# A chunked RWKV7 scan with its second head's 64-wide systems on the other half of the partitions, paired products, and square roots taken on 12 columns instead of 768

## The chip, the cores and the metric

The kernel runs on one core of one Trainium2 chip. The metric is the device time of one execution in microseconds (us); smaller is better. All numbers below are of the kernel before the change.

## The reference, cut to what matters

The whole program is a two-layer diffusion block in float32 (512 latent positions, 256 context positions, width 1024). Layer 0 mixes by windowed attention and a Hyena filter, layer 1 by RWKV7, and both have a SwiGLU. The change touches the RWKV7 recurrence and the normalisation behind it, and nothing else:

```
kk = rw_heads(k * k_k)
kk = kk / jnp.maximum(jnp.sqrt(jnp.sum(jnp.square(kk), axis=-1, keepdims=True)), 1e-12)
k_dir = k[None] * (1.0 + (a - 1.0) * k_a)
...
sa = jnp.einsum('ebhvk,ebhk->ebhv', s, kk_t)
s = s * w_t[..., None, :] - sa[..., :, None] * (kk_t * a_t)[..., None, :] + v_t[..., :, None] * k_t[..., None, :]
y = jnp.einsum('ebhvk,ebhk->ebhv', s, r_t)
...
var = jnp.mean(jnp.square(y - mean), axis=-1, keepdims=True)
yn = (y - mean) * lax.rsqrt(var + RW_GN_EPS)
```

There are 16 heads of 64 channels and two directions e (forward and backward), each over 768 positions (context, then latent).

## The kernel before, in words

A tile is a pair of heads h = 0, 1, one on partitions 0 to 63 and one on 64 to 127, so there are 8 tiles. The 768 positions are cut into 12 chunks of TC = 64, which lie in pairs: pair j = 0 to 5, and p = 0, 1 says which chunk of the pair. Inside a chunk the recurrence is a triangular system of 64 by 64, solved by doubling: blocks of 16 are inverted on POOL, then two levels (16 to 32, 32 to 64) are products on PE. What is left is a chain over the chunks.

Five engines each run a list of instructions in an order that is written out by hand and joined by semaphores (`PEM`, `DV`, `AC`, `PO` are the lists of marks). `ROUNDS` runs over (i, n, c) = (it, it+1, it+2): in one round tile i is solved and finished ("back"), tile n is prepared ("front"), and for tile c the keys are normalised. So rounds overlap three tiles. PSUM has eight banks: the back products take turns on bank pairs 0-1 and 2-3 (`BACK`), the front ones on 4-5 and 6-7 (`FRONT`). A product may start when the one two places before it in its list has been read out.

PE's list in a round, with the lines of the profile:

- `lora` L2143: `l00 l01` (and, after `w16`, `l10 l11`), 4 matmuls of 64 rows by 128 columns of the array, 384 moving columns, for direction e on the rows `H2[e]`. ACT applies tanh, POOL halves it, DVE forms the running sum `scan_e` (L2472), ACT the exponentials `ep_e en_e`.
- `squares` L2159, 24 matmuls of 64x64 each: `w16 x16 y16 w32 y32` for both directions (10 of them), then `ok obv` for both (the solved keys and values); at the round's end `BV_0 BV_1`. Head h goes to bank b+h, and chunk p has rows p and columns p of the array.
- `A_0`, `A_1` (L2169, `gram`): the system matrices of tile n; DVE masks them (`mA_e`, L2513), SP carries the blocks of 16 through DRAM to POOL and their inverses back to `XY`, which `w16` of the next round waits for.
- `m_0 m_1` (L2251), `n_0 n_1` (L2264, L2268), `r` (L2278), `yt` (L2288): transition matrices, chunk states, readout of the state, outputs from inside the chunk.
- `chain` L2198: `c0_k c1_k` for k = 1 to 10, each followed on DVE by `st0_k st1_k` (L2529). Between them stand `cg` (three matmuls of 512 columns), `K_e` (L2169), `CD_e` (L2181), and the transposes `tV tB_e tK_e` (L2150), which ACT reads out (L2384).
- `ys` (L2346), `kT_0`, `kk` (L2355), `kT_1`, `mean` (L2362), `BV_0 BV_1`, `var` (L2368).

DVE's end of a round: `ysum`, `cen`, then for tile c `kmax` (L2609), `krec` (L2611, the reciprocal of 128x768) and `kmul`, then for tile i `rec` (L2616, the reciprocal of 128x512), `f1 f2 z`. Then comes the next round's mask of `w16` (L2463). `HONES` is a 128x128 matrix of ones in two blocks of 64: its product with squares gives every channel of a head the head's sum, so the root and the reciprocal are taken on 64 equal copies.

Of the kernel before, what the change touches and what calls it, by code (L numbers as in the profile page):

```python
# [8 lines left out]
ALU = mybir.AluOpType  # L9
# [4 lines left out]
L = 512  # L14
C = 256
T = L + C
# [13 lines left out]
CH = 64  # L30
# [58 lines left out]
def hybrid_dit_kernel(nc, a, out):  # L89
# [3 lines left out]
    with ctx:  # L93
# [1744 lines left out]
        def mixes_dve(v):  # L1838
# [65 lines left out]
        OKT = WI  # L1904
# [30 lines left out]
        class Marks(dict):  # L1935
# [23 lines left out]
        DV = Marks(dve_done, (  # L1959
# [113 lines left out]
        def scan_pool(pool):  # L2073
            sub = Chain(pool, sub_step)
            for _, n, _ in ROUNDS:
# [6 lines left out]
                if n:  # L2082
                    pool.wait_ge(pe_done, PEM["obv_1", n - 1])
# [26 lines left out]
        def scan_pe(pe):  # L2110
# [739 lines left out]
```

## Time and profile before

| what | us |
|---|---|
| median of 3 runs | 2684.48 (2682.06 to 2690.17) |
| the profiled execution's own time | 2696.97 |
| its span | 2695.2 |
| the stage that the change touches, first `kk` to last `z` | 1581.4 to 2208.2 |
| one round in its middle (from `lora` to `lora`) | 71.91 |

Names in the profile are those of the memory arenas: `scan_front`, `scan_tokens`, `scan_back`, `scan_small`, and PS for PSUM. A float32 matmul of the program appears as two records of PE (a transpose as one), each with a weight load of its own; the time of a record is from its start to its modelled end, and records overlap. What a stream of them takes is read from the starts. "issue" as the end of a wait means that nothing in the trace held the engine.

### The profile page before, as it was taken

To read this page: it belongs to the slowest core of one execution; us is meant where nothing else is said; L and a number is where in the kernel's file an instruction comes from. 1 tells how busy PE (TensorE), PEld (TensorE's weight loads), DVE (VectorE), ACT (ScalarE), POOL (GpSimd) and SP (SyncE) were. 2 spreads that over 40 slices of the span, in tenths; PEclk is the share of its full clock that TensorE was granted. 3 is DMA by queue.
4 is the path that set the end of the run, shared out by engine and by line. 5 is a ranking of instruction groups with operands and counts; after the bars stand their busy time and mean duration, and the time that the engine had idled before them with its cause. 6 is when DMAs were issued, how large, how long until landed. Compare 5 with 4: busy or idle time off the path is not lost. (4 is left out here: it accounts for less than half of the span.)

```text
span 2695.2 us, 53413 instructions
## 1 busy us (share of the span) xinstructions
PE 2350.2 (87%) x23840; PEld 1946.5 (72%) x23840; DVE 1019.5 (38%) x1482; ACT 640.1 (24%) x952; POOL 836.0 (31%) x699
## 2 busy tenths in 40 slices
PE   5899977989699999999489957888888858999997
PEld 3778754555499999999269936776777746788786
DVE  4100076890400000122692045777777641200123
ACT  4110165421400000122321123333333212211111
POOL 2233200100144444343054412222222205466562
PEclk8999988989799999999599968999999978999998
DMA  5555510001021111111123411111211111222231
GB/s 219 209 203 203 209 49 17 0 31 48 16 71 62 62 62 62 56 62 48 26 79 110 138 51 39 37 40 39 40 40 38 22 64 63 77 94 93 86 98 67
DMA packets 139278, 204.26 MB, mean 76 GB/s; under 512 B 87783, under 2 KB 97511, under 8 KB 131912
## 3 DMA queue, kind: packets, MB, share of 16 engines
q1 hardware_dynamic: 139080, 201.26, 23.1%
q8 instruction: 168, 2.75, 0.4%
q14 instruction: 30, 0.25, 0.0%
HBM read 183.93 MB, written 17.30 MB: 75 GB/s over the span
## 5 line engine op out<-in xcount | busy, mean ns | idle before, releaser
L258 POOL CAST TMP_r<-WR 128x1024 fp32r<-128x1024 f32 x120 | 126.9, 1058 | 757.3 <-DMA WR<-in_ffn_w_dram 437.9
L277 PE MATMUL PS<-H_r,TMP_r 128*128 128x384 f32 (+1 forms) x1088 | 331.1, 360 | 15.1 <-DVE Y_r L492 15.1
L277 PE MATMUL PS<-Y_r,TMP_r 128*128 128x384 f32 (+1 forms) x1088 | 330.3, 358 | 3.7 <-DVE H_r L492 3.7
L260 POOL TENSOR_TENSOR WR_r<-WR,TMP_r 128x1024 fp32r<-128x1024 f32 x120 | 290.0, 2416 | 9.6
L415 DVE TENSOR_TENSOR P<-TMP,PS 128x768 f32 (+1 forms) x44 | 36.1, 821 | 563.0 <-PE PS L277 563.0
L277 PEld LDWEIGHTS PS<-H_r,TMP_r 128*128 128x128 f32 x1088 | 202.1, 190 | 33.6 <-DVE Y_r L492 17.3
L277 PEld LDWEIGHTS PS<-Y_r,TMP_r 128*128 128x128 f32 x1088 | 201.8, 190 | 19.3 <-DVE H_r L492 4.0
L277 PE MATMUL PS<-H_r,WR_r 128*128 128x384 f32 x736 | 191.6, 342 | 0.0
L268 POOL CAST TMP_r<-WR 128x1024 fp32r<-128x1024 f32 x68 | 86.4, 1271 | 322.8 <-DMA WR<-in_rw_w_rkv_dram 165.3
L270 POOL TENSOR_TENSOR WR_r<-WR,TMP_r 128x1024 fp32r<-128x1024 f32 x68 | 165.3, 2431 | 5.4
L398 ACT ACTIVATE TMP<-PS 128x768 f32<-128x768 f32 (+1 forms) x44 | 31.1, 706 | 526.5 <-PE PS L277 526.5
L588 PE MATMUL PS<-H_r,TMP_r 128*128 128x384 f32 x704 | 153.0, 340 | 3.2 <-DVE H_r L626 2.2
L2159 PE MATMUL PS<-scan_back 64*64 64x64 f32 x3840 | 122.6, 223 | 28.0 <-DVE scan_back L2463 17.5
L2159 PEld LDWEIGHTS PS<-scan_back 64*64 64x64 f32 x3840 | 119.6, 139 | 34.2 <-DVE scan_back L2463 21.8
L277 PE MATMUL PS<-Y_r,WR_r 128*128 128x512 f32 x352 | 139.4, 396 | 0.0
L277 PEld LDWEIGHTS PS<-H_r,WR_r 128*128 128x128 f32 x736 | 133.5, 189 | 0.0
L588 PEld LDWEIGHTS PS<-H_r,TMP_r 128*128 128x128 f32 x704 | 126.4, 189 | 3.8 <-DVE P L415 2.5
L1731 PE MATMUL PS<-P_r,TMP_r 128*128 128x384 f32 (+1 forms) x448 | 113.1, 344 | 1.0 <-DVE X_r L1856 1.0
L588 PE MATMUL PS<-Y_r,TMP_r 128*128 128x512 f32 x352 | 109.7, 393 | 2.4 <-DVE Y_r L626 2.4
L1622 PE MATMUL PS<-H_r,TMP_r 128*128 128x384 f32 x352 | 94.8, 352 | 8.7 <-POOL WR_r L260 8.5
L1622 PE MATMUL PS<-H_r,WR_r 128*128 128x384 f32 x352 | 92.5, 345 | 0.0
L626 DVE TENSOR_TENSOR H_r<-P,H_r 128x768 fp32r<-128x768 f32 x44 | 43.3, 1022 | 129.1 <-ACT H_r L619 129.1
(289 smaller groups left out, 4433.1 us busy)
## 6 DMA issues: line engine op xcount, KB each, us to landing
WR<-in_ffn_w_dram SPq DMA_DIRECT2D x88, 512.0 KB, 3.5
TMP<-in_mod_w_dram SPq DMA_DIRECT2D x40, 1024.0 KB, 4.9
WR<-in_down_dram SPq DMA_DIRECT2D x44, 512.0 KB, 3.6
WR<-in_mix_w_in_dram SPq DMA_DIRECT2D x24, 512.0 KB, 7.0
WR<-in_rw_w_rkv_dram SPq DMA_DIRECT2D x24, 512.0 KB, 4.2
P<-in_mod_w_dram SPq DMA_DIRECT2D x4, 2048.0 KB, 21.9
vkr_dram<-extra SPq DMA_DIRECT2D x16, 384.0 KB, 4.8
scan_front<-vkr_dram SPq DMA_DIRECT2D x16, 384.0 KB, 3.3
```

Source lines behind the costliest of these rows:

```text
L258: nc.gpsimd.tensor_copy(hi, raw).then_inc(weights_hi, 1)
L260: nc.gpsimd.tensor_tensor(lo, raw, hi.bitcast(F32), ALU.subtract).then_inc(weights_split, 1)
L268: nc.gpsimd.tensor_copy(hi, raw).then_inc(weights_hi, 1)
L270: nc.gpsimd.tensor_tensor(lo, raw, hi.bitcast(F32), ALU.subtract).then_inc(weights_split, 1)
L277: last = nc.tensor.matmul(PS[:, bank + b, 0:h1 - h0], w, x[:, h0:h1], start=k + p == 0, stop=k == CT - 1 and p == 2)
L398: nc.scalar.activation(as_halves(GATE[:, u, 0:d.n], d.n), halves(bank, d.n), ACT.Silu)\
L415: nc.vector.tensor_tensor(as_halves(dst, d.n), as_halves(GATE[:, u, 0:d.n], d.n), halves(4 * u + 2, d.n), ALU.mult).then_inc(d.unit_free, 1)
L588: last = nc.tensor.matmul(PS[:, bank, 0:h1 - h0], w[:, at:at + 128], x[:, q % 4, h0:h1], start=k + p == 0, stop=k == FT - 1 and p == 2)
L626: nc.vector.tensor_tensor(d.lo[:, q % 4, :], P[:, q % FT, 0:d.n], d.hi[:, q % 4, :].bitcast(F32), ALU.subtract).then_inc(hid_split, 1)
L1622: last = nc.tensor.matmul(PS[:, 2 * u + b, 0:HALF], w, x[:, HALF * b:HALF * b + HALF], start=k + p == 0, stop=k == CT - 1 and p == 2)
L1731: last = nc.tensor.matmul(PS[:, 2 * (t % SLOTS) + b, 0:h1 - h0], wt, x[:, k, h0:h1], start=k + p == 0, stop=k == CT - 1 and p == 2)
L2159: last = nc.tensor.matmul(PS[pr, b + h, 64 * j:64 * j + 64], lhs(pr, h, j), rhs(pr, h, j), start=True, stop=True)
```

## The change

Eight edits of the scan stage; the rest of the program is the same.

1. `lora(n, k)` makes both directions at once, with the two row halves of the array in turn.
2. For head 1 the systems of chunk p lie on the partitions of chunk 1-p (`H2[p ^ h]`), in `A_e`, `BV_e`, the solved `OO`, and the transposed keys `KINT`. For that `turned` replaces the transposes `kT_e`: 6 transposes of 64 partitions and 12 matmuls with the identity.
3. `solve` makes keys and values in one product of 128 moving columns (`oo_0 oo_1 oo_2` for `ok_e obv_e`), 48 matmuls instead of 96. `transition` does so for `m` and `r` (`mr_0 mr_1 mr_2`), `gram_keys` for the keys and readout (`KD_e`); `gram_rest` is `CK_e`.
4. `yt` and `ys` add up in PSUM: `YTS` and `ysum` go, ACT copies `ys`.
5. Sums of squares go the other way round (`turned_sums`): 128x12 and 128x8 values instead of 128x768 and 128x512. Root and reciprocal are taken of these, ACT widens them to 64 columns each (`kwide`, `vwide`), PE transposes them back (`kr`, `vr`), DVE multiplies from PSUM.
6. `ends_e first_e rate_e acc_0` move from DVE to ACT.
7. Orders: `scan_0` ahead of the `w16` masks on DVE, `scan_1` right behind them; `rt kd kt` of tile n later; `n_1` last before the chain, `cg` before `n_0`.
8. Masks of 1024 and 768 elements become four of 512, 512, 512 and 256 (`mK mD mC mL`), one set behind `st_2`, `st_3`, `st_5`, `st_6`.

```diff
         PEM = Marks(pe_done, (
...
-            (0, "c0_8 c1_8"), (1, "tK_0"), (0, "c0_9 c1_9"), (1, "tB_1"), (0, "c0_10 c1_10"), (1, "tK_1"),
-            (0, "ys"), (1, "kT_0"), (2, "kk"), (1, "kT_1"), (0, "mean"), (1, "BV_0 BV_1"), (0, "var")))
+            (1, "l00 l10"), (0, "w16_0 w16_1"), (1, "l01 l11"), (0, "x16_0 y16_0 x16_1 y16_1 w32_0 w32_1 y32_0"),
+            (1, "A_0"), (0, "y32_1 oo_0 oo_1"), (1, "A_1"), (0, "oo_2 mr_0 mr_1 cg mr_2 n_0 yt n_1"),
+            (0, "c0_1 c1_1"), (1, "KD_0"), (0, "c0_2 c1_2"), (1, "CK_0"), (0, "c0_3 c1_3"), (1, "KD_1"),
+            (0, "c0_4 c1_4"), (1, "CK_1"), (0, "c0_5 c1_5"), (1, "tV"), (0, "c0_6 c1_6"), (1, "tB_0"),
...
+            (0, "c0_10 c1_10"), (1, "kT_0"), (0, "ys"), (1, "kT_1"), (0, "mean"), (2, "kk"), (1, "BV_0"), (0, "var"),
+            (2, "kr"), (1, "BV_1"), (0, "vr")))
...
+            (0, "st0_3 st1_3"), (1, "mC_0 mL_0"), (0, "st0_4 st1_4"), (1, "accr"), (0, "st0_5 st1_5"), (1, "mK_1 mD_1"),
+            (0, "st0_6 st1_6"), (1, "mC_1 mL_1"), (0, "st0_7 st1_7 st0_8 st1_8 st0_9 st1_9 st0_10 st1_10 cen"),
...
                 for h in range(2):
-                    last = nc.tensor.matmul(PS[:, b + h, 0:HALF], w[r, :], x[r, HALF * h:HALF * h + HALF],
-                                            start=True, stop=True)
-                PEM.done(last, name, n)
+                    for e, r in enumerate(H2):
+                        last = nc.tensor.matmul(PS[:, b[e] + h, 0:HALF], w[r, :], x[r, HALF * h:HALF * h + HALF],
+                                                start=True, stop=True)
...
+            def turned(n, e):
+                name = f"kT_{e}"
                 b = front(name, n)
                 for j in range(6):
+                    c = slice(64 * j, 64 * j + 64)
+                    nc.tensor.transpose(PS[:, b, c], KIN[e][H2[0], 128 * j:128 * j + 128], ident[H2[0], H2[0]])
+                    for p in range(2):
+                        t = 128 * j + 64 * p
+                        last = nc.tensor.matmul(PS[H2[1 - p], b + 1, c], KIN[e][H2[1], t:t + 64], ident[H2[1], H2[1]],
+                                                start=True, stop=True)
...
+            def solve(i, name, turns):
+                b = back(name, i)
+                for k, (e, j) in enumerate(turns):
+                    for h in range(2):
+                        for q, qr in enumerate(H2):
+                            last = nc.tensor.matmul(PS[H2[q ^ h], b + h, 128 * k:128 * k + 128], XY[qr, 2 + e, h, j, :],
+                                                    beside(KINT[qr, e, h, j, :], BVT[qr, e, h, j, :]),
+                                                    start=True, stop=True)
...
+            def turned_sums(bank, src, groups):
+                for j in range(groups):
+                    last = nc.tensor.matmul(PS[:, bank, 2 * j:2 * j + 2], src[:, 128 * j:128 * j + 128],
+                                            HONES[:, 0:128:64], start=True, stop=True)
...
+                    pe.wait_ge(dve_done, DV["n_1", i])
+                    chain(i, 1)
...
+                    AC.done(nc.scalar.activation(KROOT, PS[:, front_bank("kk", c), 0:12], ACT.Sqrt), "kroot", c)
...
+                    act.wait_ge(dve_done, DV["krec", c])
+                    AC.done(nc.scalar.activation(KS.rearrange("p (k t) -> p k t", t=TC),
+                                                 KROOT.unsqueeze(2).broadcast_to([128, 12, TC]), ACT.Copy), "kwide", c)
...
-                    DV.done(nc.vector.reciprocal(KS, KS), "krec", c)
...
+                    DV.done(nc.vector.reciprocal(KROOT, KROOT), "krec", c)
```

At the end of a round PE's list was this (the last `c` pair, the transposes L2150, `ys` L2346, `kk` L2355, `mean` L2362, `BV` L2159, `var` L2368, and the next round's `lora` L2143):

```order
L2198 MATMUL PS<-scan_back 64x64 x4
L2150 MATMUL PS<-ident,scan_front 128x128 x6
L2346 MATMUL PS<-scan_small,scan_back 64x64 x32
L2150 MATMUL PS<-ident,scan_front 128x128 x6
L2355 MATMUL PS<-scan_front 128x384 x2
L2150 MATMUL PS<-ident,scan_front 128x128 x6
L2362 MATMUL PS<-scan_small,scan_front 128x512
L2159 MATMUL PS<-scan_tokens 64x64 x48
L2368 MATMUL PS<-scan_small,scan_front 128x512
L2143 MATMUL PS<-TMP,scan_small 128x384 x4
```

In the changed program the same place reads so (`c` L2311, `turned` L2171 and L2174, `ys` L2294, `mean` L2422, `kk` and `var` L2301, `BV_e` L2224, `kr` L2436, `vr` L2444, `lora` L2145):

```order
L2311 MATMUL PS<-scan_back 64x64 x4
L2171 MATMUL PS<-ident,scan_tokens 128x64
L2174 MATMUL PS<-ident,scan_tokens 64x64 x2
...
L2294 MATMUL PS<-scan_small,scan_back 64x64 x32
...
L2422 MATMUL PS<-scan_small,scan_front 128x512
L2301 MATMUL PS<-scan_front 128x2 x6
L2224 MATMUL PS<-scan_tokens,scan_front 64x64 x24
L2301 MATMUL PS<-scan_front,scan_small 128x2 x4
L2436 MATMUL PS<-ident,scan_front 128x128 x6
L2224 MATMUL PS<-scan_tokens,scan_front 64x64 x24
L2444 MATMUL PS<-ident,scan_small 128x128 x4
L2145 MATMUL PS<-TMP,scan_small 128x384 x4
```

The pair L2171, L2174 stands six times on each side of `ys` in place of six transposes of 128x128, `kk` has moved behind `mean`, and `kr` and `vr` are new.

DVE's list from `cen` into the next round was:

```order
L2606 SCALAR_TENSOR_TENSOR scan_small<-PS,scan_small 128x512
L2609 TENSOR_SCALAR scan_front<-scan_front 128x768
L2611 RECIPROCAL scan_front<-scan_front 128x768
L2613 TENSOR_TENSOR scan_front<-scan_front 128x768
L2616 RECIPROCAL scan_small<-scan_small 128x512
L2618 SCALAR_TENSOR_TENSOR scan_small<-scan_small,PC 128x512
L2620 SCALAR_TENSOR_TENSOR scan_small<-scan_small,PC 128x512
L2622 TENSOR_TENSOR Y<-scan_small 128x512
L2463 TENSOR_TENSOR scan_back<-PS,scan_small 128x768 x2
L2472 SCALAR_TENSOR_TENSOR scan_front<-extra,scan_front 128x768
```

and is now (`cen` L2755, `kmax` L2758, `krec` L2760, `rec` L2763, `kmul` L2766, `f1 f2 z` L2770 to L2775, `scan_e` L2589, the `w16` masks L2580):

```order
L2755 SCALAR_TENSOR_TENSOR scan_small<-PS,scan_small 128x512
L2758 TENSOR_SCALAR scan_small<-scan_small 128x12
L2760 RECIPROCAL scan_small<-scan_small 128x12
L2763 RECIPROCAL scan_small<-scan_small 128x8
L2766 TENSOR_TENSOR scan_front<-scan_front,PS 128x768
L2770 SCALAR_TENSOR_TENSOR scan_small<-scan_small,PC,PS 128x512
L2772 SCALAR_TENSOR_TENSOR scan_small<-scan_small,PC 128x512
L2775 TENSOR_TENSOR Y<-scan_small 128x512
L2589 SCALAR_TENSOR_TENSOR scan_front<-extra,scan_front 128x768
L2580 TENSOR_TENSOR scan_back<-PS,scan_small 128x768 x2
L2589 SCALAR_TENSOR_TENSOR scan_front<-extra,scan_front 128x768
```

The two long reciprocals have become short ones, `kmul` and `f1` read PSUM, and the running sum stands ahead of the masks.

## Rows read from the trace of the kernel before

**Rows 1.** Stretches of one round, then the last round; columns as headed.

```profile
core 0: us, PE busy (x) PEld busy (x) DVE busy (x) ACT busy (x) POOL busy (x), PEclk, DMA share, GB/s
1859.63:1885.98 26.35, 22.54 (x545) 19.50 (x545) 24.02 (x25) 7.73 (x10) 3.26 (x4) 0.94 0.03 8
1885.98:1906.45 20.47, 15.00 (x721) 14.20 (x722) 15.88 (x21) 3.92 (x5) 4.23 (x5) 1.00 0.15 24
1906.45:1921.63 15.18, 14.61 (x353) 10.94 (x345) 10.07 (x27) 4.44 (x6) 12.20 (x30) 1.00 0.32 91
1921.63:1927.47 5.84, 5.80 (x83) 4.25 (x82) 0.69 (x1) 5.37 (x7) 0.00 (x0) 1.00 0.50 72
1927.47:1931.54 4.07, 4.00 (x98) 3.18 (x99) 4.03 (x3) 2.97 (x5) 0.00 (x0) 1.00 0.49 45
2144.96:2208.16 63.20, 46.19 (x1306) 38.55 (x1306) 31.70 (x46) 5.75 (x8) 0.00 (x0) 0.80 0.01 3
```

**Rows 2.** The same view: five whole rounds, `lora` to `lora`.

```profile
1715.47:2073.74 358.27, 309.09 (x8922) 258.95 (x8921) 273.10 (x371) 122.12 (x150) 95.53 (x190) 0.98 0.19 37
```

**Rows 3.** Timeline of DVE: start, duration, then what.

```profile
1856.75 4.95 DVE L2611 RECIPROCAL scan_front<-scan_front 128x768 f32<-128x768 f32 x1
1862.62 3.35 DVE L2616 RECIPROCAL scan_small<-scan_small 128x512 f32<-128x512 f32 x1
1868.18 1.81 DVE L2463 TENSOR_TENSOR scan_back<-PS,scan_small 128x768 f32<-128x768 f32 x2
1869.91 1.75 DVE L2472 TENSOR_TENSOR_SCAN scan_front<-extra,scan_front 128x768 f32<-128x768 f32 x1
1909.87 0.69 DVE L2584 TENSOR_TENSOR scan_small<-PS,scan_front 128x512 f32<-128x512 f32 x1 [2.18 <-PE PS L2299]
```

**Rows 4.** Timeline of PE at the round's start: `lora`, then `w16`.

```profile
1859.63 2.84 PE L2143 MATMUL PS<-TMP,scan_small 64*128 64x384 f32 x8
1862.40 3.01 PE L2159 MATMUL PS<-scan_back,scan_tokens 64*64 64x64 f32 x96
```

**Rows 5.** Timeline of PE in the attention: scores on two row halves.

```profile
363.03 0.70 PE L735 MATMUL PS<-P 64*128 64x256 f32 x4
```

**Rows 6.** Timeline of PE, last round: `r`, and `yt`'s last record.

```profile
2174.61 1.11 PE L2278 MATMUL PS<-scan_tokens,scan_back 64*64 64x64 f32 x63
2176.99 0.27 PE L2278 MATMUL PS<-scan_tokens,scan_back 64*64 64x64 f32 x1 [1.27 <-issue]
...
2180.46 0.27 PE L2288 MATMUL PS<-scan_tokens 64*64 64x64 f32 x1 [1.38 <-issue]
```

**Rows 7.** Timeline of PE: a third of `cg`, the chain, `ys`.

```profile
1907.76 1.02 PE L2298 MATMUL PS<-TMP,scan_small 128*128 128x512 f32 x2
...
1918.46 0.87 PE L2150 MATMUL PS<-ident,scan_front 128*128 128x128 f32 x6
1919.26 0.45 PE L2198 MATMUL PS<-scan_back 64*64 64x64 f32 x8
1919.64 0.87 PE L2150 MATMUL PS<-ident,scan_front 128*128 128x128 f32 x6
1921.63 2.08 PE L2346 MATMUL PS<-scan_small,scan_back 64*64 64x64 f32 x64
```

**Rows 8.** Timelines of ACT (read-out, table load) and of POOL.

```profile
1924.55 0.81 ACT L2384 ACTIVATE scan_back<-PS 128x768 f32<-128x768 f32 x1 [0.31 <-PE PS L2150]
1925.38 1.28 ACT L2427 ACT_TABLE_LOAD   x1
...
1862.72 1.63 POOL L2081 TENSOR_SCALAR scan_front<-scan_front 128x768 f32<-128x768 f32 x2 [14.51 <-ACT scan_front L2374]
```

**Rows 9.** First tile: DVE's `mA_1`, then PE's first `w16`.

```profile
1610.71 0.96 DVE L2513 TENSOR_TENSOR scan_tokens<-PS,extra 128x768 f32<-128x768 f32 x1 [1.68 <-PE PS L2169]
1645.46 5.39 PE L2159 MATMUL PS<-scan_back,scan_tokens 64*64 64x64 f32 x96 [9.39 <-DMA scan_back<-inv_dram]
```

**Rows 10.** The stretch view again: chain to `var` of the last round.

```profile
2180.46:2200.00 19.54, 14.97 (x154) 9.69 (x155) 6.86 (x23) 1.82 (x3) 0.00 (x0) 0.66 0.01 2
```

More of the change, by code:

```diff
@@ L1977, in hybrid_dit_kernel @@
         FRONT_FREE = {"l00": (AC, "t00"), "l01": (AC, "t01"), "l10": (AC, "t10"), "l11": (AC, "t11"),
[L1978 to L1982 removed]
+                      "A_0": (DV, "mA_0"), "A_1": (DV, "mA_1"), "cg": (AC, "gt"), "KD_0": (DV, "mD_0"),
+                      "CK_0": (DV, "mL_0"), "KD_1": (DV, "mD_1"), "CK_1": (DV, "mL_1"), "kk": (AC, "kroot"),
+                      "kr": (DV, "kmul"), "BV_0": (AC, "bv_0"), "BV_1": (AC, "bv_1")}
+        BACK = "w16_0 w16_1 x16_0 y16_0 x16_1 y16_1 w32_0 w32_1 y32_0 y32_1 oo_0 oo_1 oo_2 mr_0 mr_1 mr_2 n_0 yt n_1".split()
+        BACK_FREE = {"oo_0": (AC, "oo_0"), "oo_1": (AC, "oo_1"), "oo_2": (AC, "oo_2"), "mr_0": (DV, "r_0"),
+                     "mr_1": (DV, "r_1"), "mr_2": (DV, "m5_1")}
         def front_bank(name, n):
@@ new lines, in transition @@
+            def transition(i, e):
+                name = f"mr_{e}"
+                b = back(name, i)
+                pe.wait_ge(act_done, AC[f"oo_{e}", i])
+                for j in range(4):
+                    for p, pr in enumerate(H2):
+                        for h, hr in enumerate(H2):
+                            last = nc.tensor.matmul(PS[hr, b + p, 128 * j:128 * j + 128], OO[pr, e, h, j, 0, :],
+                                                    beside(CD[pr, e, h, 0, j, :], TOKB[pr, e, j, hr]),
+                                                    start=True, stop=True)
+                PEM.done(last, name, i)
@@ new lines, in transition_rest @@
+            def transition_rest(i):
+                b = back("mr_2", i)
+                pe.wait_ge(act_done, AC["oo_2", i])
+                for e in range(2):
+                    for j in range(4, 6):
+                        at = 128 * e + 64 * (j - 4)
+                        for p, pr in enumerate(H2):
+                            for h, hr in enumerate(H2):
+                                last = nc.tensor.matmul(PS[hr, b + p, at:at + 64], OO[pr, e, h, j, 0, :],
+                                                        TOKB[pr, e, j, hr], start=True, stop=True)
+                PEM.done(last, "mr_2", i)
@@ new lines, in outputs_carried @@
+            def outputs_carried(i):
+                pe.wait_ge(dve_done, DV["st1_10", i])
+                for ch in range(NLAT):
+                    for e in range(2):
+                        was = order(e)[order(e).index(ch) - 1]
+                        at = 64 * (ch // 2)
+                        for hr in H2:
+                            last = nc.tensor.matmul(PS[hr, 2 + ch % 2, at:at + 64], NE[hr, e, was % 2, was // 2, :],
+                                                    RSTEP[hr, ch % 2, e, ch // 2, :], start=False,
+                                                    stop=ch >= NLAT - 2 and e == 1)
+                PEM.done(last, "ys", i)
@@ L2225, in scan_pe @@
[L2225 to L2232 removed]
+                        level("x16", e, "w16", Ym, Wm)
@@ L2245, in scan_pe @@
[L2245 to L2253 removed]
+                        pe.wait_ge(act_done, AC["kT_1", i])
@@ L2291, in scan_pe @@
-                    PEM.done(last, "yt", i)
-                    pe.wait_ge(dve_done, DV["r", i])
-                    chain(i, 1)
+                    solve(i, "oo_2", [(e, j) for e in range(2) for j in (4, 5)])
+                    transition(i, 0)
+                    transition(i, 1)
                     b = front("cg", i)
```

559 lines of the change are left out of this document (310 added, 249 removed), and 18 rows, old and new, of tables (AC, DV, PEM).

## The prediction

> **What bounds the kernel now.** I read, in this order, the table of stretches (who is busy when), the timelines of PE and DVE in one round (who waits for whom), and the two ends of the stage. The table cuts one round into five stretches [rows 1]. No engine is full: in the 71.9 us of the round PE is busy 62.0 us and DVE 54.7. The bound changes hands. In the first stretch (26.35 us, `lora` to the first solve) DVE is busy 24.0 us: the two reciprocals of the old round's end (4.95 and 3.35 us) run into it, and the masks of `w16` start at 1868.18, 8.55 us after `lora`, though PE had finished `w16` at 1865.4 [rows 3, 4]. From there on PE is the longer one: in the stretch from `c_1` to `ys` it is busy 14.6 of 15.2 us.
>
> In the second stretch (20.5 us) PE is busy only 15.0 us. The rest is mostly waits that nothing in the trace explains. The last round shows their pattern: products that fill all four 64x64 quadrants run at 13.5 ns a record (63 records in 1.11 us, less the last one's 0.27), yet the ends of two such waits lie 3.47 us apart (1.27 us up to 2176.99, 1.38 us up to 2180.46), with the 128 records of `yt` in between [rows 6]. So a long run of these costs 3.4 us for 128, or 26.7 ns a record, whatever the array could do. I read this as the supply of instructions. The Trainium skill (Runtime: NRT & Kernel Launch, Instruction fetch mechanics) says that instructions come in blocks of 256, which is 128 matmuls with their weight loads, and agrees; it also calls the cost mostly hidden, and there the trace differs, with 1.27 and 1.38 us each. By the page's word the sum below would lose two stalls of about 1.4 us in a round, some 22 us in eight.
>
> Five whole rounds take 358.27 us, 71.65 each [rows 2].
>
> **The change, stretch by stretch, in a middle round.** All times count from `lora`. I take 0.1 us for a hand-over between engines, 0.9 us for a DVE pass over 768 elements (two in 1.81 [rows 3]), 0.6 to 0.7 us over 512 (0.69), 0.8 us for an ACT read-out (0.81 [rows 8]), and 1.4 us for a diagonal `squares` (96 records in 3.01 [rows 4]).
>
> *`lora` to first solve: 26.35 before, 20.0 after.* Two row halves do work side by side: 4 records of 256 columns start 0.107 us apart ((0.70 - 0.38)/3) [rows 5], so eight of 384 columns take 1.6 us, not 2.84. Then tanh 0.8, POOL 0.8 (1.63 for two [rows 8]) and `scan_0` 1.75 end at 5.1; the masks of `w16` behind it end at 6.9, `scan_1` at 8.6. `x16 y16` go in turns with their freed banks until 13.5, `kin_0 ba_0` to 15.2, the `w32` masks to 17.0, `bt_0` to 17.9, `y32_0` to 18.8. PE meanwhile has `A_0` and `y32_1` until 20.0. The removed reciprocals (8.3 us) are thus worth 6.3 us here, since what replaces them is in the last stretch.
>
> *To `c_1`: 20.5 before, 19.8 after.* Solve: 96 records of 128 columns replace 192. At 13.5 ns for 64 columns they take 27 ns, 2.6 us in all against four times 1.4. But `A_1` waits for `bt_1` (23.9), `mr_1` for ACT's read of `oo_2` (27.0), and `cg`, now ahead of the states, takes about 3.05 (three parts of 1.0 us [rows 7]) and ends at 30.95. Then `mr_2`, `n_0`, `yt`, `n_1` are 352 records of the fast kind. Between 352 x 13.5 ns = 4.8 us and 352 x 26.7 = 9.4 I take 7.8, since `cg` gives the supply time for one block. `n_1` is now last, so its read-out (0.96 with two hand-overs) lies ahead of the chain: `c_1` at 39.8.
>
> *`c_1` to `ys`: 15.2 before, 18.9 after.* `cg` is gone from it. But the masks behind `st_5` (1.25 us) now free the bank for `tV`, and `tV` stands ahead of `c_6`; the same holds for `st_6`, `tB_0` and `c_7`. Each of these steps costs c 0.4, st 0.5, masks 1.0 to 1.25, transposes 0.8, together about 2.9 us, against 1.18 us for a step before (the transposes start at 1918.46 and 1919.64 [rows 7]). With the others `c_10` is at 15.0 and `kT_0`, which waits until ACT has done `kc ksq tB_1`, at 15.9. `turned` has no equal in the trace. It changes between 64*128 and 64*64 six times there and back. In the chain one such pair of changes costs what 1.18 us leaves above the work: 8 records of 30 ns and 6 of 0.10 to 0.12 leave 0.2 to 0.35 us. So `turned` takes 6 x 0.2 + 0.6 = 1.8 at least and 6 x 0.35 + 1.3 = 3.4 at most, or, if a change between shapes with the same 64 rows were free, 1.1. I take 3.0, near the upper end, because its items are short and each waits for the one before to leave the array.
>
> *`ys` to end of `mean`: 5.8 before, 6.1 after:* 2.05 (`ys` [rows 7]), 3.0 (`turned` again, which covers ACT's copy of `ys`), 1.05 (`mean`, 512 columns as a part of `cg`).
>
> *End of `mean` to the next `lora`: 4.1 before, 7.3 after.* This is the price of the short reciprocals. `cen` 0.7, `sq` 0.65 (two thirds of the elements of a read-out), table load 1.28 [rows 8], `kroot` 0.25, `bv_0` 0.75, `groot` 0.2, `kwide` 0.85, `kr` 0.85 with its hand-over, `BV_1` 0.8, `bv_1` 0.9. The next `lora` needs the bank that `bv_1` frees. `kk` and `var` (12 and 8 records of at most 0.12 us) lie beside ACT's part.
>
> Sum: 20.0 + 19.8 + 18.9 + 6.1 + 7.3 = 72.1 us against 71.9 for this round and 71.65 on average: about 0.45 us more in each of five rounds, 2.2 in all. The gains and losses of the middle rounds cancel.
>
> **The ends of the stage** do not. Before the first round, `mA_1` of tile 0 ends at 1611.7 and `w16` starts 33.8 us later (1645.46), on the blocks' way through DRAM and POOL, which the change leaves alone [rows 9]. After it there is no 4.95 us reciprocal in front of the first `scan`, less on DVE ahead of `mA_1` and twice the speed for `lora`: it comes about 6.7 us sooner, of which I keep 5.5, since PE has to be through the front of tile 0 too. The first round then takes 0.6 us more than before. The next to last has no keys to normalise: 1.5 us less. The last one (63.2 us [rows 1]) gains about 8.5: 2.6 since `f1 f2 z` and the masks of `w16` no longer wait for 3.35 us of `rec`, 3.3 in solve and states, 0.5 in the chain, 2.1 at `var` to `z` (3.35 + 0.7 less two short steps, the widening and the transposes).
>
> One term more: the granted clock. It was 0.98 over five rounds [rows 2] and 0.94 in the first stretch, where PE waits for DVE [rows 1]. With two levels, 2.4 and 1.2 GHz, a mean of 0.98 is 4% of the time at the lower one, 2.9 us of a round, and costs 1.4. After the change PE waits at more places, so I add a third of that, an estimate: 0.5 us a round, 3.5 in all.
>
> Total: -5.5 + 0.6 + 2.2 - 1.5 - 8.5 + 3.5 = -9.2 us. The profiled execution was 2696.97 us, 12.5 above the median of 2684.48; taken off the median, 2675.3 us.
>
> **Rivals.**
> - *`turned` is cheap.* If its changes of shape cost nothing, 1.1 us each: twice 1.9 us in seven rounds, 26.6 us less: 2649. For it: both shapes use 64 rows. Against it: the only change seen, of columns and rows, costs 0.2 to 0.35. Chance 0.15.
> - *No wait for instructions behind `cg`.* If the supply gets far enough ahead during `cg`, two waits of 1.4 us go in each round: 22 us less, 2653. Against it: in the last round such waits come every 128 records [rows 6], and 352 stand here. This is also what the page's word would give. Chance 0.08.
> - *Solve and value products don't spread over four quadrants.* The new placing has both row halves write to one bank at once, where the old four-quadrant products had a bank for each. Then records of 128 columns cost 54 ns instead of 27: 0.85 us on the path at `oo_2`, 0.7 at `BV_1`, in eight rounds 12.4 us more: 2688. Against it: `squares` writes so today, at 30 ns, two at a time. The Trainium skill has this as a rule (TensorEngine Tiling, Gotcha 1: different row tiles cannot access the same PSUM bank simultaneously); the trace shows two doing it in halves of a bank, and nothing here shows four. Chance 0.10.
> - *Slower: the chain with its waits pulls the clock down.* PE would stand still at `kr`, `A_1`, ahead of `c_1` and at the masks, 1 to 2 us each. If 4 us of its work in each round ran at the lower of its two levels, that is 4 us more in a round, 28 in seven, less the 3.5 in the sum: 2700. It decides from about 2.9 us a round on. For it: in the last chain, with nothing between its steps, the clock was 0.66 [rows 10]. Chance 0.15.
> - The forecast itself: 0.52.
>
> **Numbers.** What a measurement can tell from no change is about 0.3%, or 8 us: below 2676.4 and above 2692.5. My case's own range is 2662 to 2688 (1.5 us a round either way in seven rounds, 2 us at the ends), so it gives about half of itself to faster and nearly all the rest to the same. Faster 0.49 (0.15 and 0.08 of it the first two rivals), same 0.31, slower 0.20 (0.13 of it the clock, the rest the banks and my own case). Range 2650 to 2696.
>
> **What would show it.** Right: `RECIPROCAL` of 128x12 and 128x8 well below 0.5 us; `lora` at 1.6 us; solve at 27 ns a record; `turned` 3 us; `c_6` and `c_7` 2.9 us after the step before; 7 us from `mean` to `lora`; a round of 71 to 73 us; first `w16` 5 us sooner, last round 55 us. Wrong: a round below 69 us (then `turned` or the supply of instructions was overpriced) or over 74 (then look at PEclk, at `mr_1`, and at ACT between `cen` and `kr`).

## The result and the profile after

The change made the kernel slower: 2725.14 us (median of four runs, 2717.38 to 2729.26) against 2685.75 in the same rounds for the kernel before, a ratio of 1.0134 with a 95% interval of 1.0115 to 1.0153. The prediction said 2675.3, at most 2696. The interval lies clear of 1: the change costs 1.2 to 1.5%. The profiled execution took 2726.47 us with a span of 2724.5, and the mean granted clock was 0.912 (before 0.932).

The view of stretches over the same cuts as in [rows 1], then the last round from its `w16` on, then the five middle rounds as in [rows 2]:

```profile
core 0: us, PE busy (x) PEld busy (x) DVE busy (x) ACT busy (x) POOL busy (x), PEclk, DMA share, GB/s
1873.29:1894.81 21.52, 19.22 (x544) 16.78 (x545) 17.09 (x17) 9.80 (x15) 4.69 (x4) 0.96 0.03 10
1894.81:1915.30 20.49, 14.77 (x577) 11.49 (x573) 15.98 (x21) 4.28 (x5) 7.06 (x13) 1.00 0.15 22
1915.30:1935.56 20.26, 16.54 (x298) 13.93 (x299) 10.36 (x30) 5.50 (x7) 9.96 (x22) 0.83 0.39 91
1935.56:1942.96 7.40, 7.40 (x103) 5.89 (x103) 0.00 (x0) 2.22 (x3) 0.00 (x0) 0.77 0.19 20
1942.96:1951.60 8.64, 7.10 (x127) 6.17 (x126) 2.25 (x5) 5.09 (x9) 0.00 (x0) 0.70 0.01 2
...
2181.00:2238.00 57.00, 45.59 (x1159) 38.07 (x1157) 24.99 (x47) 5.93 (x9) 0.00 (x0) 0.77 0.01 3
...
1712.84:2108.77 395.93, 330.14 (x8162) 275.16 (x8161) 228.16 (x365) 135.21 (x191) 108.48 (x190) 0.88 0.17 34
```

The reader is to see two things. The five rounds hold fewer records than before (8162 against 8922) and less DVE work (228 against 273 us), and still take 37.7 us more: 79.2 each, not 71.65. And the clock of the last three stretches, 1.00 before, is now 0.83, 0.77 and 0.70. With the levels 1.2 and 2.4 GHz, 0.88 over 395.93 us is 24% of the time at the lower one, 19 us of a round. Before it was 2.9.

Where the 29.3 us between the two spans came about (the medians are 39.4 us apart, since the profiled execution of the kernel before took 12.5 us more than its median; where those 12.5 lie isn't known):

| part of the program | forecast | measured |
|---|---|---|
| up to the first middle round (1712.84 against 1715.47) | -4.9 | -2.6 |
| five middle rounds (395.93 against 358.27) | +4.7, clock term included | +37.7 |
| the last two rounds (2108.77 to the end of `z` at 2238.56; before 2073.74 to 2208.16) | -9 | -4.6 |
| behind the stage (485.9 against 487.0) | 0 | -1.1 |

The timeline of PE, the same round from `turned` on (a pair L2171, L2174 stands six times, the first three and the last one are shown):

```profile
1933.02 0.27 PE L2171 MATMUL PS<-ident,scan_tokens 64*128 64x64 f32 x1 [0.55 <-ACT scan_tokens L2472]
1933.22 0.33 PE L2174 MATMUL PS<-ident,scan_tokens 64*64 64x64 f32 x4
1933.49 0.27 PE L2171 MATMUL PS<-ident,scan_tokens 64*128 64x64 f32 x1
...
1935.55 0.27 PE L2174 MATMUL PS<-ident,scan_tokens 64*64 64x64 f32 x2
...
1935.67 3.21 PE L2294 MATMUL PS<-scan_small,scan_back 64*64 64x64 f32 x63
...
1947.62 1.51 PE L2436 MATMUL PS<-ident,scan_front 128*128 128x128 f32 x6 [1.54 <-ACT scan_front L2548]
1949.07 1.56 PE L2224 MATMUL PS<-scan_tokens,scan_front 64*64 64x64 f32 x48
1950.56 1.11 PE L2444 MATMUL PS<-ident,scan_small 128*128 128x128 f32 x4
```

`turned` takes 2.6 us, a pair every 0.46 us, and `ys` behind it 3.21 us where it took 2.08 [rows 7]. `kr`, `BV_1` and `vr` behind the wait run at half speed (`BV_0`, the same work, took 0.93 us at 1944.17). The waits of PE over the five rounds, with their total, number and longest:

```profile
PE PS L2153 <- DVE scan_tokens L2629: 8.9, 5, 1.9
PE PS L2162 <- DVE scan_back L2580: 8.8, 10, 0.9
PE PS L2185 <- DVE scan_front L2602: 7.6, 5, 1.5
PE PS L2153 <- DVE scan_front L2638: 6.8, 5, 1.4
PE PS L2436 <- ACT scan_front L2548: 6.6, 5, 1.5
PE PS L2283 <- issue: 5.7, 4, 1.7
PE PS L2311 <- DVE scan_back L2663: 5.3, 5, 1.1
```

None is longer than 1.9 us, and these seven are 49.7 us in all, 10 us of a round (13.1 with the smaller ones). L2153 is `tV` and `tB_0` at the masks, L2185 is `A_1` at `bt_1`, L2436 is `kr` at the widening, L2311 is `c_1` at `n_1`. Waits of this length stood in the kernel before too, 9.6 us of a round in all, and its clock was 0.98. The longest, from the same view over its five rounds:

```profile
PE PS L2268 <- issue: 9.2, 6, 2.2
```

So the waits alone don't explain the clock.

### The profile page after: what moved, and what is told of

The parts are those of the page before. It is cut to its first block and busy times, and to the rows that moved or that the text cites. A ratio compares the mean times of both kernels' runs of the same rounds, so it can differ in the third digit from the quotient of the medians.

```text
span 2724.5 us, 51046 instructions
## 1 busy us (share of the span) xinstructions
PE 2374.1 (87%) x22624; PEld 1965.6 (72%) x22624; DVE 945.4 (35%) x1475; ACT 661.4 (24%) x1016; POOL 850.0 (31%) x699
## 5 line engine op out<-in xcount | busy, mean ns | idle before, releaser
L2085 POOL TENSOR_SCALAR scan_front<-scan_front 128x768 f32<-128x768 f32 x32 | 36.1, 1147 | 249.9 <-ACT scan_front L2451 249.9
L1622 PE MATMUL PS<-Y_r,TMP_r 128*128 128x384 f32 x352 | 91.0, 339 | 0.0
L343 PE MATMUL PS<-Hraw,WR 128*128 128x384 f32 x256 | 85.6, 498 | 5.8 <-DVE Hraw L1425 5.8
```

The lines of the kernel that those rows point to most:

```text
L343: last = nc.tensor.matmul(PS[:, 2 * s + h, 0:HALF], WR[:, s, k, :], outproj.rhs(k)[:, HALF * h:HALF * h + HALF], start=k == 0, stop=k == C ...
L1622: last = nc.tensor.matmul(PS[:, 2 * u + b, 0:HALF], w, x[:, HALF * b:HALF * b + HALF], start=k + p == 0, stop=k == CT - 1 and p == 2)
L2085: PO.done(nc.gpsimd.tensor_scalar(x, x, 0.5, 0.5, ALU.mult, ALU.add), f"s{e}{k}", n)
```

## The experiments

All ratios are to the kernel before, timed beside each kernel. Its median there lay between 2683.66 and 2691.03 us, so a difference of two medians from different groups of runs can be off by up to 7 us. Where it matters, the difference of the ratios is given beside it. "Five rounds" is the stretch from one `lora` to the fifth after it, at the place of [rows 2].

**Masks one step earlier.** The masks of direction 1 stand one step of the chain sooner, so the transposes shouldn't wait for them. To make room I put `accr` behind `st_6`.

```diff
-            (0, "st0_4 st1_4"), (1, "accr"), (0, "st0_5 st1_5"), (1, "mK_1 mD_1"), (0, "st0_6 st1_6"), (1, "mC_1 mL_1")
+            (0, "st0_4 st1_4"), (1, "mK_1 mD_1"), (0, "st0_5 st1_5"), (1, "mC_1 mL_1"), (0, "st0_6 st1_6"), (1, "accr")
```

> The changed kernel with the masks of KD_1 and CK_1 on DVE one chain step earlier (behind st_4 and st_5, where their products already stand ready) and accr behind st_6. Theory of the lost order: tV and tB_0 no longer wait 1.9 and 1.4 us for the masks, 3 us a round, about 20 us in all: near 2705. Theory that these waits are hidden by something that comes later (ACT's row of copies): within 5 us of the changed kernel, 2720 to 2730.

Measured: 2738.02 us, 1.0173 [1.0132, 1.0213]. A miss, by a side effect of the edit: the waits of `tV` and `tB_0` for the masks fell from 15.7 us in five rounds to 3.3, but a new one stood at the head of the list.

```profile
PE PS L2171 <- ACT scan_tokens L2472: 14.9, 5, 4.7
```

`accr` frees what the load of the next tile's keys waits for; ACT's `kc` stands in front of the transposed tiles and came late (ACT waited up to 4.0 us for that load, 11.6 us in five rounds). The clock of the five rounds was 0.83. So the experiment was repeated without that.

**The same, with `accr` left ahead of `st_5`.**

```diff
+            (1, "accr mK_1 mD_1"), (0, "st0_5 st1_5"), (1, "mC_1 mL_1"), (0, "st0_6 st1_6")
```

> The changed kernel with the masks of KD_1 and CK_1 one chain step earlier, and accr left in its place ahead of them. The run before this one moved accr behind st_6; in its trace PE waits for ACT ahead of turned, up to 4.7 us, 14.9 in five rounds, where the changed kernel has 1.4, so the keys' load that waits for accr came late. Theory of the lost order: tV and tB_0 wait 2 to 3 us less a round, 12 to 20 us in all: 2705 to 2713. Theory that something later takes it up (the clock, or ACT ahead of turned, since now that is reached sooner): 2720 or more.

Measured: 2711.77 us, 1.0088 [1.0063, 1.0113], and 77.1 us a round; the theory of the lost order was right. The order of the masks costs the changed kernel 13 us, about 2 us a round.

**`turned` with its shapes apart.** First the six transposes, then the twelve products: one change of shape instead of eleven, the same work.

```diff
                     nc.tensor.transpose(PS[:, b, c], KIN[e][H2[0], 128 * j:128 * j + 128], ident[H2[0], H2[0]])
+                for j in range(6):
+                    c = slice(64 * j, 64 * j + 64)
                     for p in range(2):
```

> The changed kernel with the six transposes of turned first and its twelve products after them, the same work with one change of array shape instead of eleven inside it. Theory of the shape changes: turned falls from 2.8 to about 1.2 us, 3.2 us a round, 7 rounds, and the clock of ys behind it is higher: 22 to 30 us less, 2696 to 2704. Theory that turned is slow by its many small products: no more than 5 us less.

Measured: 2678.07 us, 0.9966 [0.9953, 0.9979]; 72.4 us a round, clock 0.93. That is 47 us less than the changed kernel. In the timeline both parts together now take 1.4 us:

```profile
1840.16 0.58 PE L2171 MATMUL PS<-ident,scan_tokens 64*128 64x64 f32 x6
1840.67 0.91 PE L2176 MATMUL PS<-ident,scan_tokens 64*64 64x64 f32 x24
```

The step itself became some 1.4 us shorter, twice in a round. The round became 6.8 us shorter. So more than half of what `turned` cost did not lie in `turned`.

**`turned` on four quadrants.** 24 products of 64x64 with the identity for each direction, no transposes, so there is one shape all the way from the chain to `mean`.

```diff
-                    nc.tensor.transpose(PS[:, b, c], KIN[e][H2[0], 128 * j:128 * j + 128], ident[H2[0], H2[0]])
                     for p in range(2):
                         t = 128 * j + 64 * p
+                        for h, hr in enumerate(H2):
+                            last = nc.tensor.matmul(PS[H2[p ^ h], b + h, c], KIN[e][hr, t:t + 64], ident[hr, hr],
```

> The changed kernel with turned made of 24 products of 64x64 only, for both heads, in turn on the four quadrants, with no change of shape and no transposes. More products and more instructions (48 records instead of 30). Theory of the shape changes: about 0.9 us instead of 2.8, 3.8 us a round and the clock of ys back: like the batched form or 3 to 6 us better, 2672 to 2680. Theory that small products as such lower the clock: the time of turned falls but ys stays at 3 us, 2690 to 2705.

Measured: 2674.47 us, 0.9942 [0.9921, 0.9963]; 71.9 us a round, clock 0.93. `turned` takes 0.86 us (46 of its 48 records) and `ys` is back at 1.97.

**The placement undone.** Keys by six transposes of 128x128 as before, the solve and the values with both heads on their chunk's partitions; the rest of the change stays.

```diff
-last = nc.tensor.matmul(PS[H2[q ^ h], b + h, 128 * k:128 * k + 128], XY[qr, 2 + e, h, j, :],
+last = nc.tensor.matmul(PS[qr, b + h, 128 * k:128 * k + 128], XY[qr, 2 + e, h, j, :],
```

> The changed kernel with both heads' systems on the partitions of their own chunk again: keys by six transposes of 128x128 (0.8 us) instead of turned (2.8 us), solve and value products on the diagonal. Theory from the working: 4.1 us less around ys, 0.85 at oo_2 and 0.65 at BV_1 more, and a better clock for ys: 2.6 to 4 us a round less, 18 to 28 us: 2697 to 2707. Theory that the four quadrants carry their weight: no change or slower, 2725 or more.

Measured: 2686.19 us, 0.9989 [0.9975, 1.0002]; 73.2 us a round, clock 0.95: better than expected by 10 us or more, and the clock came back with `turned` gone. The solve shows the placement's own worth. The groups of the five rounds in the changed kernel, then here (busy us and mean ns of a record behind the bar):

```profile
L2233 PE MATMUL PS<-scan_back 64*64 64x128 f32 x480 | 16.5, 272 | 1.4 <-DVE scan_back L2584 1.4
```

```profile
L2221 PE MATMUL PS<-scan_back 64*64 64x128 f32 x480 | 28.1, 269 | 0.0
```

That is 34 against 59 ns a record, 2.3 us of a round. With a good `turned` the placement is worth 12 us (2686.19 to 2674.47; 13 by the ratios).

**Four quadrants and the masks.** Both edits above together.

> The two edits together: turned on four quadrants, and the masks of KD_1 and CK_1 one step earlier. If the waits for the masks are worth 2 to 3 us a round when nothing else covers them: 2655 to 2665, clear of the kernel before. If ACT's row of copies ahead of turned takes them up: 2670 to 2680.

Measured: 2650.48 us, 0.9850 [0.9830, 0.9870]; 69.4 us a round, clock 0.94. It beats both kernels.

**Length or clock.** The four-quadrant kernel, with its `turned` brought back to the length that it has in the changed kernel, but by dense work.

```diff
                 b = front(name, n)
+                for h in range(2):
+                    nc.tensor.matmul(PS[:, b + h, 0:512], ident[:, :], RUN[:, 0:512], start=True, stop=True)
```

> The kernel of e7_quad (2674.5) with two products of 128 rows by 512 columns put ahead of each turned, at the place in PE's list where turned stood longer. A third of cg shows 1.02 us for one such product, so each turned is about 2.0 us longer, as in the changed kernel (2.8 against 0.86 us), but the added time is filled densely. If what the changed kernel lost beyond the length of turned is the clock, pulled down by thin items, the five middle rounds take 71.9 + 3.9 = 75.8 us with a clock of 0.93 to 0.95 there, and the kernel 2697 to 2706. If length on this path alone explains the changed kernel, it comes out at 2718 to 2730 with rounds of 79 us.

Measured: 2700.01 us, 1.0065 [1.0041, 1.0088]. Its five rounds, then those of the four-quadrant kernel:

```profile
1703.36:2080.62 377.26, 311.82 (x8382) 254.69 (x8381) 227.95 (x365) 134.40 (x191) 109.67 (x190) 0.93 0.17 35
```

```profile
1704.67:2064.13 359.46, 290.90 (x8342) 246.36 (x8341) 227.68 (x365) 134.69 (x191) 110.65 (x190) 0.93 0.19 37
```

The same clock, 3.6 us more a round, 25.5 us in all: that is the length of `turned`. The lengths match: in the changed kernel 2.64 us lie between the starts of the first and the last record of a `turned` at full clock, here 2.62. The changed kernel has this length in another form and is slower by another 25.1 us, with a clock of 0.88. By the ratios the two shares are 33 and 19 us, by the five rounds alone 17.8 and 18.7. So of the 51 us that its `turned` costs, about half is length, and 19 to 25 us are clock.

The clock is lost behind `turned`. From its start to the next `lora`, one round of the changed kernel, then one of this kernel:

```profile
1933.02:1951.60 18.58, 17.03 (x252) 13.87 (x253) 2.25 (x5) 7.96 (x13) 0.00 (x0) 0.77 0.18 19
```

```profile
1915.26:1931.84 16.58, 15.04 (x297) 11.07 (x297) 2.25 (x5) 7.96 (x13) 0.00 (x0) 0.91 0.17 17
```

Over the five rounds this stretch takes 19.8 us a round at a clock of 0.71 in the changed kernel and 16.9 us at 0.88 here: 3.0 of the 3.7 us by which their rounds differ. The waits are the same, 13.1 us of a round in both and 13.6 in the four-quadrant kernel, so they don't make this difference.

**Idle products in the waits of the changed kernel.** Two of 512 columns ahead of `c_1`, four of 384 ahead of `kr`; they write to a bank that is overwritten next.

```diff
+                        fill(front("KD_0", n), 0, 512, 2)
                     pe.wait_ge(dve_done, DV["n_1", i])
...
+                    fill(b, 0, 384, 4)
                     pe.wait_ge(act_done, AC["kwide", c])
```

> The changed kernel with products that nobody reads added on PE in two places where it stands still: 2 of 512 columns ahead of the first chain step, 4 of 384 ahead of kr. Theory of the clock: the stretches behind these two places, at 0.70 and 0.73 now, go up to 0.9 or more, a round loses 1.5 to 3 us: 2702 to 2715. The stretch of ys, which has turned ahead of it, stays low. Theory that the waits alone are the loss: 2725 to 2735.

Measured: 2735.46 us, 1.0171 [1.0143, 1.0199]. The clock rose from 0.88 to 0.90, but the four products took 4.5 us in a wait of 1.5 us (round from 1875.41), so the test says little. Repeated with one product of 512 columns at each place:

> The changed kernel (2725), and one idle product of 128 rows by 512 columns (1.0 us) in the wait of 1.1 us ahead of c_1 and one in the wait of 1.5 us ahead of kr, as in e13_bothfill. e6_fill3 did this with too much work. If the low clock of the changed kernel comes from light stretches at any place, some of it comes back: the same two products gave e8_both 12 us, and here 19 us of a 79 us round run at the lower level, so 2695 to 2713. If the clock there belongs to turned alone, nothing comes back: 2720 to 2732.

Measured: 2716.63 us, 1.0109 [1.0080, 1.0138]; 78.7 us a round, clock 0.90. That is 8.5 us less than the changed kernel by the medians and 7 by the ratios, between the two expectations; the intervals of the two ratios overlap, so the gain isn't shown beyond doubt. In the round at 1870.78 the clock is 1.00 up to 1913, 0.84 up to 1935, and 0.65 from there to the next `lora`. Behind the second `turned` it is as low as ever.

**The same two products in the best kernel.**

> The kernel of e8_both (2650.5) with one idle product of 128 rows by 512 columns (1.0 us) in the wait of 1.1 us ahead of c_1, and one in the wait of 1.5 us ahead of kr. Both fit into their wait at full clock. The middle rounds of e8_both have a clock of 0.94, 4.2 us of 69.4 at the lower level, so at most 2 us a round can come back: 2638 to 2650 if the waits cause it, 2651 to 2658 if the fillers only delay what stands behind them.

Measured: 2638.72 us, 0.9809 [0.9792, 0.9825]. Work that nothing uses, 2 us of a round, makes the kernel 12 us faster (11 by the ratios). The expectation had the room wrong by a factor of two: a clock of 0.94 over 69.4 us is 8.3 us at the lower level, not 4.2, so 4.2 us a round could come back, and 2.5 did. The five rounds, and the end of one (L2436 is now the idle product, L2439 `kr`, L2447 `vr`):

```profile
1699.93:2034.44 334.51, 285.46 (x8361) 236.34 (x8361) 226.85 (x366) 134.40 (x191) 110.31 (x190) 0.99 0.20 40
```

```profile
1828.76 1.12 PE L2436 MATMUL PS<-extra,ident 128*128 128x512 f32 x2
1830.35 0.88 PE L2439 MATMUL PS<-ident,scan_front 128*128 128x128 f32 x6 [0.46 <-ACT scan_front L2551]
1831.16 0.93 PE L2224 MATMUL PS<-scan_tokens,scan_front 64*64 64x64 f32 x48
1832.02 0.66 PE L2447 MATMUL PS<-ident,scan_small 128*128 128x128 f32 x4
```

A round is 66.9 us at a clock of 0.99. `kr` takes 0.88 instead of 1.51, `BV_1` 0.93 instead of 1.56, and the next `lora` 1.56 instead of 2.17, against the same round of the kernel without the two products.

**The old way to the roots**, on the four-quadrant kernel.

```diff
-                    PEM.done(turned_sums(b, KS, 6), "kk", c)
+                        last = nc.tensor.matmul(PS[:, b + h, 0:HALF], HONES, KS[:, HALF * h:HALF * h + HALF],
...
-                    DV.done(nc.vector.reciprocal(KROOT, KROOT), "krec", c)
+                    DV.done(nc.vector.reciprocal(KS, KS), "krec", c)
```

> The kernel of e7_quad (2674.5) with the old way to the roots: sums of squares by the matrix of ones on 768 and 512 columns, roots and reciprocals of 128x768 and 128x512, no widening and no transposes back. By the forecast's own steps the short way gains 6.3 us at the round's start and costs 3.2 between mean and lora, 3.1 us net a round, plus 4.7 in the last: 27 us, so 2693 to 2710 here, with the reciprocals (4.95 and 3.35 us) ahead of the next round's w16 masks. Rival: the end of the round, with four waits of PE and a low clock there (8.6 us from mean to lora in place of 7.3), eats the gain: 2670 to 2682.

Measured: 2712.09 us, 1.0098 [1.0079, 1.0118]; 78.1 us a round. The short reciprocals are worth 37.6 us (42 by the ratios), not 27. PE waits 7.4 us for the `w16` masks there, and what follows runs slowly; the timeline, then the stretches:

```profile
1870.71 8.53 PE L2163 MATMUL PS<-scan_back 64*64 64x64 f32 x192 [7.35 <-DVE scan_back L2564]
```

```profile
1857.36:1870.71 13.35, 6.00 (x112) 4.34 (x113) 13.21 (x9) 5.55 (x7) 3.25 (x4) 0.84 0.04 12
1870.71:1879.06 8.35, 8.35 (x192) 8.35 (x194) 5.24 (x5) 4.47 (x9) 0.00 (x0) 0.64 0.01 2
```

**`lora` alone.** The kernel before with only the first edit of the change.

```diff
+            def lora(n, k):
+                for h in range(2):
+                    for e, r in enumerate(H2):
+                        last = nc.tensor.matmul(PS[:, b[e] + h, 0:HALF], w[r, :], x[r, HALF * h:HALF * h + HALF],
```

> The kernel before with one part of the change alone: lora makes both directions with the row halves in turn (1.6 us for eight records instead of 2.84), with ACT's and POOL's order to match. DVE is full in the first stretch (24 of 26 us) and its scan stands behind the w16 masks, so nothing waits for lora: 2682 to 2690, no change. Rival: the front of the round starts 1.2 us sooner in every round, 2674 to 2679.

Measured: 2695.62 us, 1.0042 [1.0027, 1.0056]: slower, which neither theory allowed. PE got through its part sooner, stood still 4.6 us for the same masks instead of 1.1, and then ran slowly; and two operations of DVE became longer. The second is the larger part: 1.0 us in the round shown. From the first of the 192 records behind the wait to the next product it is 7.6 us here, and it was 7.2 in the kernel before, at a clock of 0.76; that leaves 0.4 us to the slow clock. Together this is the 1.4 us by which a round grew. DVE's timeline (`f2` and `z`), PE's, and the stretch:

```profile
1857.69 1.22 DVE L2619 SCALAR_TENSOR_TENSOR scan_small<-scan_small,PC 128x512 f32<-128x512 f32 x1
1858.94 1.19 DVE L2621 TENSOR_TENSOR Y<-scan_small 128x512 f32<-128x512 f32 x1
```

```profile
1861.15 7.77 PE L2159 MATMUL PS<-scan_back 64*64 64x64 f32 x192 [4.62 <-DVE scan_back L2462]
```

```profile
1861.15:1868.74 7.59, 7.59 (x193) 7.59 (x194) 5.24 (x5) 1.58 (x2) 0.00 (x0) 0.71 0.02 4
```

**The wait filled**, with three idle products of 512 columns behind the second `lora`.

> The kernel of e11_lora (2695.6), and in the 4.6 us in which PE stands still for the w16 masks three idle products of 128 rows by 512 columns (3 us), behind the second lora. They shorten no wait. In e11_lora the 192 records of x16 and y16 behind that wait took 7.6 us at a clock of 0.71. If the wait itself brings the clock down, they run at full speed here (about 6.1 us) and the kernel is back at 2682 to 2689. If something else in that order costs the 12 us, it stays at 2693 to 2699.

Measured: 2691.78 us, 1.0024 [1.0008, 1.0040], between the two expectations, and its interval overlaps that of the run before. The clock of the five rounds went from 0.95 to 0.99, and the 192 records took 6.3 us instead of 7.8. Still `f2` and `z` took 1.22 and 1.19 us.

**POOL out of DVE's way.** POOL's second pair of halvings waits for `scan_0`.

```diff
+                        if (e, k) == (0, 1):
+                            pool.wait_ge(dve_done, DV["scan_0", n])
```

> The kernel of e12_lfill (2691.8), and POOL's halving of the second pair waits until scan_0 is done. In e12_lfill it lies beside f2 and z on DVE, which take 1.22 and 1.19 us instead of 0.75 and 0.69, and DVE's w16 masks are what PE waits for. If that overlap is what is left of the 12 us of e11_lora, f2 and z are back at 0.75 and 0.69 and the kernel at 2682 to 2687. If it isn't, 2689 to 2694.

Measured: 2692.76 us, 1.0017 [0.9999, 1.0035]. `f2` and `z` are back at 0.75 and 0.69, and a middle round at 71.7 us, what it was before. The kernel isn't faster than the one with the wait filled, though, and missed its expectation. What is left, 6 us by the medians, is at the edge of the noise (the interval just takes in 1). In the traces it lies mostly in the last two rounds: 138.4 us from `lora` to the end of `z`, 134.4 before. The waits for issue there are 10.4 us against 8.5. Why they are longer is open.

**Both lessons in the best kernel:** POOL's second pair waits for `scan_1`, and the two idle products stay.

> The kernel of e13_bothfill (2638.7), and POOL's halving of the second pair waits for scan_1, so that only scan_0 still has a halving beside it. scan_1 takes 1.75 us instead of 2.0 to 2.4 in every round: 0.3 to 0.6 us earlier on DVE for seven rounds, 2634 to 2638. If rate and ba now come too late, 2640 to 2645.

Measured: 2637.81 us, 0.9820 [0.9796, 0.9845]: the same as without the edit of POOL. The second scan takes 1.74 us instead of 2.03, as expected, but the kernel gains nothing from it that could be told from noise.

## Why the prediction was wrong

**The step that failed** is the one headed "one term more: the granted clock". It took the 2.9 us of a round at the lower level and added a third, 0.5 us of cost a round. Measured were 19 us of a round at the lower level, 15 more than forecast. At half speed that costs up to 7.6 us a round, and the five rounds were 6.6 us each over the forecast. The length of `turned` isn't part of the failure: the sum had it, at 3.0 us each.

The rival "the chain with its waits pulls the clock down" named the low clock, gave it 2700 us and a chance of 0.15, and had the waits as its cause. It was half right. By the clocks of the five rounds, 19 us of a round are at the lower level in the changed kernel, 10 in the four-quadrant one (and 11 with dense work of the old length ahead of its `turned`), 8 with the masks earlier as well, and 1 with the two idle products on top. The first step, 9 us, leaves the waits as they are (13.1 and 13.6 us of a round). It goes with the alternating shapes of `turned`, which the prediction had priced as length alone. The other 9 us, for which the rival had 4, go with waits that are shortened or filled.

**The stretches**, in the order of the prediction, for this round of 78.3 us:

- *`lora` to the first solve:* 20.0 forecast, 21.5 measured. The first `lora` took 2.29 us, at the lower level, where 1.6 was forecast (the second took 1.56), and the two scans 2.37 and 2.00 instead of 1.75.
- *To `c_1`:* 19.8 against 20.5. Records of 128 columns come 34 ns apart over the five rounds, 27 where they run undisturbed (30 in 1.04 us, less the last one's 0.27). The rival of the banks is out. The rival without waits for instructions is out too: they are there with up to 1.7 us.
- *`c_1` to `ys`:* 18.9 against 20.3. `turned` at 2.6 us was priced rightly (3.0), and "cheap" is out in the form it has here. The masks that hold up `tV` and `tB_0` were seen, with waits of 1.7 and 1.4 us. What came on top is the lower clock in part of the stretch (six transposes in 1.54 us instead of 0.87).
- *`ys` to `mean`:* 6.1 against 7.4: `ys` took 3.21, not 2.05.
- *`mean` to `lora`:* 7.3 against 8.6: `kr`, `BV_1`, `vr` at the lower level, 4.2 us together where 2.5 would do (0.88, 0.93, 0.66 in the best kernel).

So most of the single durations held, at full clock (the scans beside POOL didn't), and the sum failed because a clock of 1.00 was carried over from the old kernel into stretches whose filling the change had altered.

**The short reciprocals** were the change's best part and were undervalued, at 27 us against 38 to 42, in part for the same reason: the stall that they remove also cost clock behind it (0.64 over the 8.35 us after it, 0.87 over the five rounds against 0.93). They took what the forecast had allowed them, in the changed kernel:

```profile
1867.82 0.23 DVE L2760 RECIPROCAL scan_small<-scan_small 128x12 f32<-128x12 f32 x1
1868.47 0.20 DVE L2763 RECIPROCAL scan_small<-scan_small 128x8 f32<-128x8 f32 x1 [0.43 <-ACT scan_small L2544]
```

**The ends:** the first `w16` came 7.2 us sooner (5.5 forecast), but the first round then took 4.5 us more than before, where 0.6 was forecast. The last two rounds gained 4.6 us instead of 9 to 10, with a clock of 0.84 over both (before 0.91).

**By parts of the change**, from the runs: roots -38 to -42 us, placement -12, interleaved shapes in `turned` +51, order of the masks +13 (24 where `turned` is good). They don't add up to the whole, since each shifts the clock of the others.

## What to carry to other kernels

A PE stretch that gets thinner, or shorter next to a wait, can cost clock in what stands behind it: price it with the granted clock of the rows behind it, and test with dense idle work of the same length whether a loss is length or clock. Don't alternate array shapes item by item; sort the items by shape, or find a form in which all have one shape. Where waits of 1 to 1.5 us can't be removed, an idle product that just fits into them may pay for itself; one that doesn't fit costs its overhang.

## What the runs showed of the hardware

- The clock went to its lower level with no wait above 1.9 us in the round: 0.70 to 0.83 over the last 36 us. The kernel before had waits of up to 2.2 us and a clock of 0.98, and the same waits with a sorted or four-quadrant `turned` gave 0.93. Two products of 1 us each brought it from 0.94 to 0.99 in the best kernel, and from 0.88 to 0.90 in the changed one.
- A change between 64x128 and 64x64 shapes cost about 0.12 us: the five records of a pair took 0.46 us with two changes, and 0.23 (1.36 / 6) when sorted.
- DVE and POOL slow each other. The running sum took 1.75 us alone and up to 2.37 beside POOL's halving, of which two took 3.06 us instead of 1.63:

```profile
1877.47 2.37 DVE L2589 TENSOR_TENSOR_SCAN scan_front<-extra,scan_front 128x768 f32<-128x768 f32 x1 [1.81 <-POOL scan_front L2085]
...
1881.03 3.06 POOL L2085 TENSOR_SCALAR scan_front<-scan_front 128x768 f32<-128x768 f32 x2 [2.80 <-ACT scan_front L2451]
```

  `f2` and `z` showed it too (0.75 and 0.69 to 1.22 and 1.19). A reciprocal of 3.35 us beside the same halving stayed at 3.35 [rows 3, 8], and the masks, which read one operand from PSUM, at 1.8, here in the run with POOL's wait:

```profile
1863.42 1.82 DVE L2471 TENSOR_TENSOR scan_back<-scan_back,PS 128x768 f32<-128x768 f32 x2
...
1863.66 1.63 POOL L2083 TENSOR_SCALAR scan_front<-scan_front 128x768 f32<-128x768 f32 x2 [7.47 <-DVE scan_front L2476]
```

  The Trainium skill (SBUF — State Buffer, Who interferes with whom) says that a DVE instruction with two inputs in SBUF contends with a GpSimd instruction that reads SBUF, and that one with at most one SBUF input doesn't, outside the two-port modes; these rows agree.
- Four-quadrant products of 128 columns, with both row halves writing to one bank, came every 34 ns over the five rounds and every 27 undisturbed, against 59 ns where both heads stand on the same two quadrants.
- Waits for issue stand in all these kernels, here of up to 1.7 us. They differ from kernel to kernel (8.5 and 10.4 us in the last two rounds of the kernel before and of the one with POOL's wait). What moves them wasn't tested.
